# Order of the gate's second half on TensorE, and of the next head's preparation on VectorE

## The reference, cut to what matters

```python
def second_block(x, p, ...):
    for i in range(DEPTH):                       # DEPTH = 2
        mix = ssd_mixer(x, ...) if i % 2 == 0 else hgrn2_mixer(x, ...)
        h = layer_norm(DEEPNORM_ALPHA * x + mix, ...)
        h = layer_norm(DEEPNORM_ALPHA * h + sq_relu_mlp(h, ...), ...)
        x = h + jax.nn.sigmoid(h @ ple_w_gate[i]) * (p[i] @ ple_w_proj[i])
    return x

def hgrn2_mixer(u, w_in, lb, norm_w, w_out):
    q, fz, v, g = jnp.split(u @ w_in, 4, axis=-1)
    log_f = jnp.logaddexp(jnp.log(lb), jnp.log1p(-lb) + jax.nn.log_sigmoid(fz))
    k = (1.0 - lb) * jax.nn.sigmoid(-fz)
    # per chunk of 64, step by step: o = sum of decayed scores * v + q * exp(b) @ state; then
    # state = exp(b_last) * state + (k * exp(b_last - b))^T v
    return (rms_norm(o) * silu(g)) @ w_out
```

## Time and profile before

| | |
|---|---|
| median of 3 runs | 2925.8 us (2922.55 to 2927.01) |
| the profiled execution, own time | 2920.26 us |
| its span | 2918.5 us |
| PE busy | 2812.9 us, 96% of the span, 13058 matmuls |
| DVE, POOL, ACT busy | 1733.6, 1732.9 and 791.1 us |
| share of PE in the chain that ended last | 81%, DVE 9%, DVE's waits for itself 4% |
| recurrence (first to last L1091 of a head) | 2158.2 to 2414.4 us, seven heads, and the last to 2450 |
| gate 0, gate 1 | end at 2135 and at 2914 us |

### The profile page before, as it was taken

How to read it: one execution, slowest core, us unless ns; L and a number is a source line. 1 busy time by engine, 2 the same in 40 slices (tenths; PEclk the granted TensorE clock), 3 DMA queues, 4 the chain that set the end, 5 groups by cost and what they waited for, 6 DMA issues and landing times.

```text
span 2918.5 us, 36566 instructions
## 1 busy us (share of the span) xinstructions
PE 2812.9 (96%) x13058; PEld 2293.9 (79%) x13058; DVE 1733.6 (59%) x1974; ACT 791.1 (27%) x1299; POOL 1732.9 (59%) x984
## 2 busy tenths in 40 slices
PE   9999999999999999989999999999899998999998
PEld 7778788887787888867776778888777777788887
DVE  7886666337867665276655566073566665842635
ACT  3433222113333222035555121020222222310202
POOL 6785666665966666654343557666553333666663
PEclk9999999999999999999999999999999999999999
DMA  4102232332022222321111223322221111232321
GB/s 154 58 30 75 92 101 94 106 102 76 23 66 92 95 95 101 108 81 58 66 65 44 80 75 106 101 94 94 80 85 58 58 58 51 87 101 94 101 94 58
DMA packets 66481, 237.40 MB, mean 81 GB/s; under 512 B 7264, under 2 KB 7520, under 8 KB 66336
## 3 DMA queue, kind: packets, MB, share of 16 engines
q1 hardware_dynamic: 65504, 234.00, 24.1%
q10 hardware_dynamic: 832, 1.51, 0.2%
HBM read 233.38 MB, written 2.10 MB: 81 GB/s over the span
## 4 chain that ended last, share of the span: by engine, by line
PE 81%; DVE 9%; DVEq 4%; issue 3%; ACT 2%; DMA 0%; POOL 0%; ACTq 0%; SPq 0%
PE ps L476 24%; PE ps L482 23%; PE ps L479 23%; PE ps L1106 2%; DVE qw L2449 1%; PE ps L875 1%; PE ps L635 1%; DVEq L2340 1%; DVEq L2451 1%; PE ps L1142 1%; DVE ps L1755 1%; PE ps L878 1%; DVE xres L2341 1%; PE ps L945 0%; PE ps L605 0%
## 5 line engine op out<-in xcount | busy, mean ns | idle before, releaser
L411 POOL TENSOR_SCALAR w_hi<-w_raw 128x1024 fp32r<-128x1024 f32 x437 | 482.9, 1105 | 1122.7 <-PE ps L476 1038.3
L413 POOL TENSOR_TENSOR w_lo<-w_raw,w_hi 128x1024 fp32r<-128x1024 f32 x437 | 1100.4, 2518 | 36.5
L476 PE MATMUL ps<-x_hi,w_hi 128*128 128x512 f32 x1864 | 747.1, 401 | 27.2 <-POOL w_lo L413 5.8
L482 PE MATMUL ps<-x_hi,w_lo 128*128 128x512 f32 x1864 | 731.4, 392 | 0.0
L479 PE MATMUL ps<-x_lo,w_hi 128*128 128x512 f32 x1864 | 730.6, 392 | 0.0
L476 PEld LDWEIGHTS ps<-x_hi,w_hi 128*128 128x128 f32 x1864 | 353.6, 190 | 115.8 <-issue 19.4
L479 PEld LDWEIGHTS ps<-x_lo,w_hi 128*128 128x128 f32 x1864 | 353.5, 190 | 75.5 <-issue 4.3
L482 PEld LDWEIGHTS ps<-x_hi,w_lo 128*128 128x128 f32 x1864 | 352.7, 189 | 75.5
L476 PE MATMUL ps<-a_hi,w_hi 128*128 128x512 f32 x512 | 200.0, 391 | 0.0
L482 PE MATMUL ps<-a_hi,w_lo 128*128 128x512 f32 x512 | 199.2, 389 | 0.0
L479 PE MATMUL ps<-a_lo,w_hi 128*128 128x512 f32 x512 | 199.2, 389 | 0.0
(11 more groups left out here) (422 smaller groups left out, 4745.3 us busy)
## 6 DMA issues: line engine op xcount, KB each, us to landing
w_raw<-wts SPq DMA_DIRECT2D x437, 512.0 KB, 3.2
xres<-xT SPq DMA_DIRECT2D x2, 1024.0 KB, 8.7
outT<-xres SPq DMA_DIRECT2D x8, 256.0 KB, 2.0
pf<-pT ACTq DMA_DIRECT2D x2, 512.0 KB, 3.7
prm<-prm SPq DMA_DIRECT2D x1, 452.0 KB, 3.7
lev<-levels ACTq DMA_DIRECT2D x1, 384.0 KB, 3.0
wtmp<-pos SPq DMA_DIRECT2D x1, 128.0 KB, 2.8
ident<-identity SPq DMA_DIRECT2D x1, 64.0 KB, 10.6
```

The costliest lines, as they stand in the source:

```text
L411: nc.gpsimd.tensor_scalar(w_hi[:, s, :], w_raw[:, s, :], 1.0, 0.0, ALU.mult, ALU.add).then_inc(w_rounded[s], 1)
L413: nc.gpsimd.tensor_tensor(w_lo[:, s, :], w_raw[:, s, :], w_hi[:, s, :].bitcast(F32), ALU.subtract).then_inc(w_split[s], 1)
L476: mm = nc.tensor.matmul(out, whi, xhi, start=first, stop=False)
L482: return nc.tensor.matmul(out, wlo, xhi, start=False, stop=last)
```

## The change

Two orders change, one on PE and one on DVE; no arithmetic is added or taken away, and no buffer moves.

1. In the second half of each gate the p product of tile 4 is made without a `bank2` before it (it writes bank 5), then, behind `bank2(0)`, the gate product of tile 4; then `bank2(1)`, the p product and the gate product of tile 5; then the p products of tiles 6 and 7, and last their gate products. Block 5 is given back after the p product of tile 7, as before, but two gate products now come before that.
2. In the recurrence `prepare(h + 1)` moves from behind level 5's masked copy, and the two `first_chains` from behind the widenings of levels 6 and 7, to behind the widening of level 7, in this order.

```diff
             def gate(L):
                 pe.wait_ge(p_split, L * KP + KP)
-                for q in range(2):
-                    s = block_in((Q0, B_PG[L] + 5 * q))
-                    for mm4 in range(4):
-                        if q or mm4 < 3:
-                            bank2(mm4)
-                        else:
-                            pe.wait_ge(p_round, (L + 1) * (KP + 1))
...
-                    passed.append(s)
-                    if q == 0:
-                        bank2(3)
-                        together(GX[:3], Q0, B_PG[L] + 1, L * 3 * KD + KD, 2 * L + 1)
-                    for mm4 in range(3 if q == 0 else 0, 4):
...
+                def side(q, mm4, s):
+                    for kt in range(KP):
+                        c = (mm4 * KP + kt) * P
+                        mm = three(ps[GP[q][mm4]][:, :], ...)
+                    mm.then_inc(pp_done, 1)
+                def gated(q, mm4):
+                    s = block_in((Q0, B_PG[L] + 5 * q + 1 + mm4))
+                    for kt in range(KD):
+                        mm = three(ps[GX[mm4]][:, :], ...)
+                    mm.then_inc(acc_ready, 1)
+                    passed.append(s)
...
+                gated(0, 3)
+                s = block_in((Q0, B_PG[L] + 5))
+                side(1, 0, s)
+                bank2(0)
+                gated(1, 0)
+                bank2(1)
+                side(1, 1, s)
+                gated(1, 1)
+                for mm4 in (2, 3):
+                    bank2(mm4)
+                    side(1, mm4, s)
+                passed.append(s)
+                gated(1, 2)
+                gated(1, 3)
...
                     if h and 1 <= v <= 4:
                         finish(h - 1, v - 1)
-                    if v == 5 and h + 1 < HH:
-                        prepare(h + 1)
-                    if v >= 6 and h + 1 < HH:
-                        first_chains(h + 1, 2 * (v - 6))
+                if h + 1 < HH:
+                    prepare(h + 1)
+                    first_chains(h + 1, 0)
+                    first_chains(h + 1, 2)
```

More of the change, by code:

```diff
@@ new lines, in side @@
+                def side(q, mm4, s):
+                    for kt in range(KP):
+                        c = (mm4 * KP + kt) * P
+                        mm = three(ps[GP[q][mm4]][:, :], w_hi[:, s, c:c + P], w_lo[:, s, c:c + P], p_hi[:, kt, :], p_lo[:, kt, :],
+                                   kt == 0, kt == KP - 1)
+                    mm.then_inc(pp_done, 1)
+                def gated(q, mm4):
+                    s = block_in((Q0, B_PG[L] + 5 * q + 1 + mm4))
+                    for kt in range(KD):
+                        mm = three(ps[GX[mm4]][:, :], w_hi[:, s, kt * P:(kt + 1) * P], w_lo[:, s, kt * P:(kt + 1) * P],
+                                   x_hi[:, kt, :], x_lo[:, kt, :], kt == 0, kt == KD - 1)
+                    mm.then_inc(acc_ready, 1)
+                    passed.append(s)
@@ new lines, in gate @@
+                s = block_in((Q0, B_PG[L]))
+                bank2(0)
+                side(0, 0, s)
+                row_factors(2 * L + 1)
+                for mm4 in (1, 2):
+                    bank2(mm4)
+                    side(0, mm4, s)
+                pe.wait_ge(p_round, (L + 1) * (KP + 1))
+                side(0, 3, s)
+                passed.append(s)
+                bank2(3)
+                together(GX[:3], Q0, B_PG[L] + 1, L * 3 * KD + KD, 2 * L + 1)
+                gated(0, 3)
```

## The result

| | before | changed |
|---|---|---|
| median of 5 runs | 2924.23 us (2919.15 to 2927.01) | 2900.54 us (2898.95 to 2906.53) |
| ratio, with its 95% interval | | 0.9924 (0.9909 to 0.9939) |
| profiled execution, own time | 2920.26 us | 2901.63 us |
| its span | 2918.5 us | 2899.8 us |

The changed kernel is faster: 23.7 us by the medians, 18.6 by the profiled executions. The forecast was 23.0 less, at 2902.8.

The account below looks back on a forecast made before the run. PE, busy in 96% of the span, was taken to bound the kernel; 8.5 (gate 0) + 3.2 (gate 1) + 6.5 (level 6) + 4.8 (level 7) = 23.0 us off 2925.8 gave 2902.8. The range was 2897.5 to 2911.5.

Parts of the forecast that it names:

- Gate 0 and gate 1: Second halves of the gates: waits for DVE's multiplications go, one for block 6 comes; 8.5 and 3.2 us won.
- Block 9: Gate 0: block 9, split into block 5's later-freed slot, is done by 2120.4, wanted at 2121.1; 0.7 us to spare.
- Level 6: Recurrence: without `prepare` before level 6's widening, PE's wait before L1126 goes; 0.95 us a head, 6.5 in all.
- Level 7 and the tie: Recurrence, level 7: DVE's L2450 starts 0.03 us before POOL's L411 and isn't held up; 0.68 us a head, 4.8 in all.
- behind gate 0: Start of the stage after gate 0: present value taken, bounded by 1.2 us gained and 2.7 lost.
- rival C: Gates and following projections: waits move to blocks split by POOL; 11.3 us won if all comes back, 2914.5; chance 0.06.
- Rival B: Gates: the clock still falls after the new wait, 1.7 us each, two cost 3.4; 2906.2 us; chance 0.07.
- Rival D: Next head's L1091 waits for late preparation once DVE's tail grows by 3.5 us; 2932 us or more; chance 0.03.
- A: Recurrence, level 7: the tie goes to POOL, L2450 still takes 1.28 us; 18.2 us won, 2907.6; chance 0.18.

Follow-up runs that it names:

- e1: Only the gates' new order against the kernel before, VectorE's order in the recurrence as before: 2918.0 us, ratio 0.9975.
- e3: Kernel before with only the two `first_chains` moved behind level 7's widening; gates and `prepare` as before: 2920.92 us, ratio 0.9989.
- e5: Changed kernel plus a copy of 128 x 8 values on DVE before level 7's widening, letting POOL go first: 2907.31 us, ratio 0.9939.
- e8: e4 with, in gate 0 from tile 4 on, each tile's rounding and low part right behind its addition: 2894.53 us, ratio 0.9901.
- e2: Only the recurrence's later preparation and chains against the kernel before, gates as before: 2914.22 us, ratio 0.9966.
- e6: Changed kernel plus one unused reciprocal of 128 x 512 on DVE before each of the seven late preparations: 2899.18 us, ratio 0.9914.
- e7: Changed kernel plus two unused reciprocals of 128 x 512 on DVE before each late preparation: 2904.42 us in one execution.
- e9: Changed kernel run again unaltered, beside the kernel before on the same chip: 2897.52 us, ratio 0.9909.
- e4: Changed kernel with blocks 5 and 6 of each gate swapped and tile 4's gate product before its p product: 2901.5 us, ratio 0.9914.

## Why the prediction was right, point by point

**Gate 0 and gate 1** (8.5 and 3.2 forecast, 8.4 and 3.1 measured; in e1 the gates have the same lengths). The forecast counted 120 matmuls of 0.227 us and one new wait of 1.2, and the trace has just this: the wait for block 6 shows as 1.05 and 1.06 us, which is 1.2 of lost slot, and no `bank2` is waited for. Block 9 is in time.

**Level 6** (0.95 a head and 6.5 in all forecast). The stretch from L1119 to L1126 went from 3.07 to 2.10 us in head 4, 0.97, and by 6.6 in the seven heads.

**Level 7 and the tie** (0.68 a head, DVE first). From L1126 to L1131 2.52 became 1.82, 0.70, and 4.8 in the seven heads. That the tie goes to DVE rested on a margin of 0.03 us; it came out at 0.01 to 0.02, and went as forecast in all seven heads. e3 takes the term alone, e5 loses it again (4.7). That e3's heads met the forecast to the tenth is in part chance: 4.1 of the 4.8 stand in the stretch that the forecast was made from, and the rest behind L1131.

**Mis-sized: the heads by 0.8.** Of this 0.1 is in the two stretches above. Behind L1131 there was a gain that the sum didn't have: from there to L1142 it takes 2.25 us where it took 2.35, 0.7 in all. The first matmuls behind a wait run slower than in a full stream: the L1149 group takes 0.70 us behind a wait and 0.59 without one. The experiments bear it out. In every one of the seven heads that stretch takes 2.34 to 2.36 us in the kernels with a wait before L1131 (before, e1, e5) and 2.25 or 2.26 in all the others, and e5 brings back wait and slow start together. Likewise L1126 to L1131 takes 1.93 in e3, where L1126 still follows a wait, and 1.82 in the changed kernel.

**Mis-sized: behind gate 0, by 0.8 the other way.** I took the present value, between -1.2 and +2.7. Two waits (1.59 us, 1.9 of lost slots) stand where one of 1.04 (1.2) did. The rows above show where it comes from: POOL goes on splitting, and tile 7's low part takes 1.52 us beside an L411 where it took 0.68. That is what the bound of 2.7 stood for, DVE held up by POOL, with an L411 in place of an L413. e8 removes both waits by taking the low parts earlier, where no split holds them up (0.75 us each); how much of it is the order and how much the shorter low parts isn't separated. PE waits for no block there, so rival C didn't happen.

**Rival B, and what a fall costs.** The clock didn't fall in the second half of a gate in any kernel with the changed gate (all but before, e2 and e3), as forecast. The prediction put a fall at half of its length, 1.7 us. Gate 0 before the change bears that out, 1.6 us, since no wait came behind it; e3 shows that the fall in gate 1 had cost nothing, since PE had to wait for DVE anyway. The forecast didn't depend on it, since it was made from the ends of the stage, which hold waits and low clock together. In the changed gates no wait follows that could cover a fall, so there I would still count 1.7; no run shows it.

**Rival D's threshold was too near.** "3.5 us are left" was the distance from the end of all of DVE's work, chains too, to the next L1091. The timeline of the changed kernel has 2.5 there: the chains (L2458) end at 2327.46. `prepare` had been put at 1.46 us, and behind the widening, beside POOL's splits, it takes 4.4 (2321.60 to 2325.98). But only `qw` has to be there, 4.0 us ahead, and held-up time isn't work. e6 and e7 put the room at about 6.7 us.

**The range.** Its upper end, 2911.5, isn't the sum that stands beside it (2902.8 + 2.7 is 2905.5); 2911.0, with A and B together, is. The measured time lies well below both.

**What stays open.** Why the start of the kernel varies between executions (60 to 78 matmuls in the first 30 us) wasn't tried. It isn't all of the 5.2 us of the first row: e1 has 74 matmuls there and reaches gate 0 as late, at 2103.55, and e8 has 60 and is at 2099.56. Since e9 is the same program, and is there at 2096.88, it isn't the change. The 1.0 us between head 7 and gate 1 lies inside the 3.6 us by which two executions of one program differed there. The stages give 22.8 us for 23.0 forecast, but two errors of 0.8 cancel in it, the heads' and the one behind gate 0: that is luck. The agreement of the median with the forecast to 2.3 us is better than the runs' own spread (7.6 us) and deserves no credit beyond the stage table.

## What to carry to other kernels

Work that only has to be ready a stage later shouldn't stand in front of what the bounding engine waits for next: moved behind it, it cost nothing here, and a filler of known length in its place shows how much room is left, which a timeline does not when the work in question is held up by another engine.

When PE is brought forward, look at what hands over to the next stage: of the 8.4 us won in gate 0, 0.8 was lost at the next stage's start, because an engine that had been idle there now held another up, until the low parts were taken at once (e8, with e4's order 3 us better than the change as made).

Compare traces stage by stage; the end-to-end difference of two executions holds several us that neither program caused.

## What the runs showed of the hardware that I had not expected

A lead of 0.01 us decides between DVE's multiplication and POOL's split. In the changed kernel and in e2 to e4 and e6 to e9, seven heads each, the multiplication at level 7 starts 0.01 to 0.02 us ahead and takes 0.42 us; before the change, in e1 and in e5 it starts 0.04 to 0.06 behind and takes 1.26 to 1.28, 0.85 more. Nothing between was run.

A stretch of some 3.4 us at half of the granted clock cost nothing where PE waited for DVE anyway (gate 1, 31.66 us with it and 31.67 without) and about 1.6 us where nothing was waited for behind it (gate 0 before the change). Its coming isn't fixed by the code: the changed kernel had a granted clock of 0.83 in its first 30 us, and 0.94 when it was profiled again (e9). And e3's gate 1, with waits of 1.96 and 1.15 us, had no fall, where before a wait of 1.98 was followed by one.

Two reciprocals, 6.79 us of DVE work in each head, cost 0.1 us a head, because a reciprocal isn't held up by POOL (3.35 us beside a split and without one) while the scalings of the preparation are (1.06 and 2.61 us, and 0.39 and 0.48 without).
